# Constant products until the first operands, first two weight tiles by halves, x's last quarter behind tile 8's weights, its sum one tile later

## What is computed

```
mk, mv = rms_norm(mem, g) @ w_k, rms_norm(mem, g) @ w_v        # 256 memory tokens
x = x + token_mix(rms_norm(x))      # one input projection, convolution and gated linear attention, one output projection
x = x + cross_attn(rms_norm(x), mk, mv)
x = x + w_down @ relu(w_up @ rms_norm(x))**2
y = rms_norm(x)
```

## Time and profile before

| what | us |
|---|---|
| median of 3 runs | 1456.31 (1456.04 to 1456.56) |
| the profiled execution: its time, its span | 1456.2, 1454.5 |
| TensorE busy | 1437.2 (99%) |
| VectorE, ScalarE, GpSimd busy | 602.8, 458.0, 376.0 |

### The profile page before, as it was taken

The page is one execution under the profiler, slowest core; times in us unless marked ns, Lnnn a source line. Parts: engine busy times, 40 slices in busy tenths (PEclk is TensorE's granted clock), DMA queues, the critical chain, the costliest instruction groups (busy, mean ns, idle before and its releaser), DMA issues.

```text
span 1454.5 us, 22506 instructions
## 1 busy us (share of the span) xinstructions
PE 1437.2 (99%) x9501; PEld 1408.8 (97%) x9501; DVE 602.8 (41%) x688; ACT 458.0 (31%) x619; POOL 376.0 (26%) x296
## 2 busy tenths in 40 slices
PE   7999999999999999999999999999999999999998
PEld 7999999998999999889999999999999999999997
DVE  5669999987533555623322111221112211122124
ACT  7522253447522443312232200222002210023224
POOL 6642231125322211003222222222222222222220
PEclk9999999999999999999999999999999999999999
DMA  8511511002523411771111111111111111111113
GB/s 338 165 52 45 58 46 42 30 30 73 207 94 114 153 42 44 247 267 44 48 47 52 44 47 54 44 43 44 58 43 43 43 44 57 44 43 43 44 43 117
DMA packets 47357, 114.06 MB, mean 78 GB/s; under 512 B 7720, under 2 KB 23352, under 8 KB 45888
## 3 DMA queue, kind: packets, MB, share of 16 engines
q1 hardware_dynamic: 47296, 113.17, 24.3%
HBM read 100.85 MB, written 12.30 MB: 78 GB/s over the span
## 4 chain that ended last, share of the span: by engine, by line
PE 96%; DVE 3%; DMA 0%; ACT 0%; issue 0%; SPq 0%; DVEq 0%; ACTq 0%
PE ps L1214 59%; PE ps L1315 14%; PE ps L1609 5%; PE ps L1332 3%; PE m L1285 2%; PE ps L1643 2%; PE ps L1741 1%; PE ps L1562 1%; PE m L1522 1%; PE ps L1351 1%; DVE ps L1903 1%; PE ps L1622 1%; PE m L1437 1%; PE m L1586 1%; PE ps L1553 1%; PE m L1535 1%
## 5 line engine op out<-in xcount | busy, mean ns | idle before, releaser
L620 POOL TENSOR_TENSOR w_split<-w_raw,w_split 128x512 fp32r<-128x512 f32 x232 | 319.2, 1397 | 1041.6 <-ACT w_split L694 1041.5
L1214 PE MATMUL ps<-a_op,w_split 128*128 128x344 f32 x3168 | 499.4, 319 | 0.0
L1214 PEld LDWEIGHTS ps<-a_op,w_split 128*128 128x128 f32 x3168 | 497.8, 188 | 0.5 <-issue 0.5
L1214 PE MATMUL ps<-b_op,w_split 128*128 128x344 f32 x2304 | 362.6, 319 | 0.0
L1214 PEld LDWEIGHTS ps<-b_op,w_split 128*128 128x128 f32 x2304 | 361.7, 188 | 0.2
L1315 PE MATMUL ps<-a_op,w_split 128*128 128x344 f32 x1440 | 233.2, 321 | 0.0
L1315 PEld LDWEIGHTS ps<-a_op,w_split 128*128 128x128 f32 x1440 | 226.5, 188 | 1.7 <-issue 1.4
L694 ACT ACTIVATE w_split<-w_raw 128x1024 fp32r<-128x1024 f32 x117 | 122.7, 1051 | 255.2 <-PE ps L1214 246.0
L1903 DVE SCALAR_TENSOR_TENSOR ps<-conv_in,par,ps 128x1024 f32<-128x1024 f32 x116 | 149.7, 1291 | 3.6
L2289 DVE SCALAR_TENSOR_TENSOR tmp<-ps,rstd 128x1032 f32<-128x1032 f32 x32 | 39.5, 1233 | 215.1 <-PE ps L1214 203.2
L2299 DVE TENSOR_TENSOR x_res<-x_res,ps 128x1032 f32 x24 | 29.5, 1230 | 230.8 <-PE ps L1214 230.8
(11 more groups left out here) (255 smaller groups left out, 1100.7 us busy)
## 6 DMA issues: line engine op xcount, KB each, us to landing
w_raw<-in_wt SPq DMA_DIRECT2D x117, 512.0 KB, 3.5
cache_b<-in_cache_v SPq DMA_DIRECT2D x8, 1024.0 KB, 12.0
x_in<-in_x SPq DMA_DIRECT2D x4, 1032.0 KB, 9.2
x_spill<-x_res SPq DMA_DIRECT2D x8, 516.0 KB, 2.6
w_more<-in_wt SPq DMA_DIRECT2D x8, 512.0 KB, 7.1
cache_a<-in_cache_k SPq DMA_DIRECT2D x2, 2048.0 KB, 11.2
cache_b<-in_cache_k SPq DMA_DIRECT2D x2, 2048.0 KB, 11.9
x_res<-in_x SPq DMA_DIRECT2D x1, 3096.0 KB, 11.0
```

Of the source, the lines that this page charges most:

```text
L620: gp.tensor_tensor(split(t, slot)[:, 1, part, :], src, split(t, slot)[:, 0, part, :].bitcast(F32), ALU.subtract).then_inc(w_low_done, 1)
L1214: last = pe.matmul(ps[:, c0 // CB, 0:w], w_split[:, slot, wp, k, :], src[:, k, xp, c0:c0 + w], start=(k == 0 and j == 0), stop=(k == KT - ...
```

## The change

1. TensorE does eleven products of two constant tiles (ones and ident, 128x128, plain fp32) before the first real one. Their result is not read.
2. Tile 0's weights are loaded in two halves, with the parameters, and the memory's two halves between them; before, par, the whole of tile 0 and the memory's halves stood in this order. ScalarE copies tile 0's and tile 1's high parts in halves, with pieces of the memory's operand between them; a new semaphore, first_high, counts the first halves, and GpSimd starts tile 1's first half on it. VectorE makes tile 0's second half after four pieces of the memory's operand instead of three.
3. x's last quarter is issued after tile 8's weights instead of tile 7's, and ScalarE copies tile 8's high part before it squares x's pieces 6 and 7.
4. `x_sums` stands after tile 9 instead of tile 8, and ScalarE copies tile 12's high part before `norm_x` instead of after.

```
+            sp.dma_start(w_raw[:, 0, 0:KT // 2, :], WT[0][:, 0:KT // 2, :]).then_inc(first_half_loaded, 16)
             sp.dma_start(par[:, :], a["par"]).then_inc(params_loaded, 16)
...
-            load_w(0, 0, False)
-            for i in range(2):
-                sp.dma_start(m_raw[:, 4 * i:4 * i + 4, :], a["mem"][:, 4 * i:4 * i + 4, :]).then_inc(m_part[i], 16)
+            sp.dma_start(m_raw[:, 0:4, :], a["mem"][:, 0:4, :]).then_inc(m_part[0], 16)
+            sp.dma_start(w_raw[:, 0, KT // 2:KT, :], WT[0][:, KT // 2:KT, :]).then_inc(w_loaded[0], 16)
+            sp.dma_start(m_raw[:, 4:8, :], a["mem"][:, 4:8, :]).then_inc(m_part[1], 16)
...
-                if 5 <= t < 8:
-                    load_x(t - 4)
+                if t in (5, 6, 8):
+                    load_x((5, 6, 8).index(t) + 1)
...
-                gp.wait_ge(w_high_done, t + 1)
                 for k in (0, KT // 2):
+                    if isinstance(t, int) and t == 1 and k == 0:
+                        gp.wait_ge(first_high, 2)
+                    else:
+                        gp.wait_ge(w_high_done, t + 1)
...
-            w_high(0, 0)
+            def half_high(t, half):
+                part = slice(half * KT // 2, (half + 1) * KT // 2)
+                act.activation(w_split[:, t, 0, part, :], w_raw[:, t, part, :], ACT.Copy).then_inc((first_high, w_high_done)[half], 1)
...
+            act.wait_ge(first_half_loaded, 16)
+            half_high(0, 0)
             act.wait_ge(params_loaded, 16)
...
+            act.wait_ge(m_part[0], 16)
+            mem_high(0, 1, 2, 3)
+            act.wait_ge(w_loaded[0], 16)
+            half_high(0, 1)
+            act.wait_ge(m_part[1], 16)
+            mem_high(4, 5)
+            act.wait_ge(w_loaded[1], 16)
+            half_high(1, 0)
+            mem_high(6, 7)
+            half_high(1, 1)
             w_high(2, 0)
...
             square_x(5)
             w_high(7, 1)
+            w_high(8, 0)
             square_x(6)
-            w_high(8, 0)
             square_x(7)
-            for t in range(9, 12):
+            for t in range(9, 13):
                 w_high(t, t % 2)
             norm_x()
-            w_high(12, 0)
...
             pe.wait_ge(consts_ready, 1)
+            for _ in range(11):
+                pe.matmul(M[1][:, 0:P], ones[:, :], ident[:, :], start=True, stop=True)
             for n_kv in range(T_IN):
                 kv_product(n_kv)
                 if n_kv == 2:
                     sums(1, 0, MEM)
-                if n_kv == 8:
+                if n_kv == 9:
                     x_sums()
...
-            dve.wait_ge(w_high_done, 1)
+            dve.wait_ge(first_high, 1)
             first_low(0)
             for k in range(KT):
-                if k == 3:
+                if k == 4:
+                    dve.wait_ge(w_high_done, 1)
                     first_low(KT // 2)
```

More of the change, by code:

```diff
@@ L244, in build @@
         w_high_done = sem("w_high_done")
+        first_high = sem("first_high")
+        first_half_loaded = sem("first_half_loaded")
         w_low_done = sem("w_low_done")
@@ L709, in _, with mem_high @@
             act.activation(small[:, 129:130], small[:, 128:129], ACT.Sqrt)
-            w_high(0, 0)
-            act.wait_ge(params_loaded, 16)
[L712 to L717, removed]
+            def half_high(t, half):
+                part = slice(half * KT // 2, (half + 1) * KT // 2)
+                act.activation(w_split[:, t, 0, part, :], w_raw[:, t, part, :], ACT.Copy).then_inc((first_high, w_high_done)[half], 1)
+            def mem_high(*ks):
+                for k in ks:
+                    act.activation(m_op[:, k, 0, :], m_raw[:, k, :], ACT.Copy,
+                                   scale=par[:, G_MEM + k:G_MEM + k + 1]).then_inc(operand_high, 1)
+            act.wait_ge(first_half_loaded, 16)
+            half_high(0, 0)
+            act.wait_ge(params_loaded, 16)
+            act.wait_ge(m_part[0], 16)
[8 more added lines that the diff above has]
+            half_high(1, 1)
             w_high(2, 0)
```

## The result

The changed kernel takes 1462.75 us (median of 6 runs, 1461.72 to 1463.08) against 1456.43 for the kernel before on the same chip (6 runs, 1456.04 to 1457.17): a ratio of 1.0041, interval 1.0032 to 1.0051, 6.3 us slower. The prediction was 1457.5, at most 1458.8. The profiled execution took 1462.9.

What follows compares the result with a forecast made beforehand. TensorE bounds the kernel, busy 1437.2 of 1454.5 us. Terms: 0 (constants) - 0.74 (clock, first operand) + 2.8 (x_sums behind tile 9) - 0.84 (VectorE's slack) = +1.3 with rounding, so 1457.5 us, range 1455.3 to 1458.8.

Steps and rivals of the forecast that it cites:

- GpSimd begins tile 1's low part at about 10.0 instead of 11.05 (first_high): Before the memory's sum: GpSimd starts tile 1 earlier, its second half done at 12.7, so tile 1 ends at 14.5.
- It lands at about 5.92: Start: the memory's first half, with 256 KB less queued before it, lands 0.64 us earlier, at 5.92 instead of 6.56.
- The eleven constant products. ... I cost them at nothing: Start: the products take 2.5 to 4.9 us, hidden in TensorE's wait for its first operands; cost 0.
- Between 60 us and the end I find no other change: After tile 16 begins: nothing more gained or lost, so the shift at tile 16 counts for the whole kernel.
- The memory's sum as the gate at 18.1: After tile 2: VectorE's reduction of the memory's squares ends at 18.1, so TensorE waits 0.8 us there.
- g: How much earlier than before TensorE gets past the memory's sum; above 2.0 us needed for a faster kernel.
- the weights rival: New wait for weights at tile 7 or 9, or x's last quarter: 0.3 to 1.5 us above forecast; chance 0.12.
- the same time: At the memory's sum: with the clock not raised, TensorE would arrive at 18.2, against a sum ready at 18.1.
- The late sum: x_sums after tile 9 begins at 38.4 instead of 36.29, delaying VectorE's row and kv_evac(7) by 2.1 us.
- VectorE's slack: Before kv_evac(7), ahead of tile 16: VectorE is idle 0.84 us, from 58.12 to 58.96, which absorbs that much delay.
- Tile 8's weights: x's last quarter behind them makes them ready 1.1 us earlier, no wait; otherwise 0.2 us would be lost at tile 8.
- the one of 0.74: Term for clock and earlier first operand: TensorE leaves the memory's sum 0.74 us earlier, 18.1 instead of 18.84.

Runs made afterwards that it cites:

- Experiment 5: The changed kernel with GpSimd's first half of tile 1 waiting for all of the memory's low pieces: 1460.02 us, ratio to before 1.0028.
- experiment 9: The kernel before with tile 0 loaded by two half-size transfers, one after the other: 1457.93 us, ratio 1.0009.
- experiment 6: The kernel before with tile 0's load in halves, parameters and memory's first half between; ScalarE copies tile 0 whole: 1458.30 us, ratio 1.0014.
- experiment 1: The kernel before with the eleven constant products alone: 1457.19 us, ratio 1.0005.
- experiment 11: The kernel before with 88 already-met TensorE waits ahead of the first product: 1457.27 us, ratio 1.0005.
- experiment 2: The kernel before with only x's last quarter behind tile 8's weights and x_sums after tile 9: 1458.07 us, ratio 1.0012.
- experiment 12: The changed kernel with its loads as in the kernel before, tile 0 whole: 1461.62 us, ratio to before 1.0039.
- experiment 3: The changed kernel without the constant products and the edits on x's last quarter and x_sums: 1459.16 us, ratio to before 1.0015.
- experiment 4: The changed kernel with x_sums back after tile 8 and tile 12's copy back behind norm_x: 1461.25 us, ratio to before 1.0028.
- experiment 7: The kernel before with eleven constant products and x's last quarter and its squares behind tile 8's weights: 1457.21 us, ratio 1.0006.
- experiment 10: The kernel before with three 512-column constant products and x's last quarter behind tile 8's weights: 1455.72 us, ratio 0.9995.

## Why the prediction was wrong, by its own steps

- **"GpSimd begins tile 1's low part at about 10.0 instead of 11.05 (first_high)", costed as a gain, is the step that failed most.** It let GpSimd subtract while VectorE still had pieces 6 and 7 to do: 1.28 and 1.50 us instead of 0.48 each. GpSimd in fact began at 11.34, but VectorE's last two pieces, at 11.61, were later still; by the prediction's own times (ScalarE's pieces 6 and 7 from 9.8 to 10.6) they would have met too. TensorE starved for it and its clock fell. Experiment 5 takes the overlap away and is 2.7 us faster, of which about 2.0 are the edit's: 0.7 of idle time between pieces and 1.3 of clock (27 matmuls in 4.6 us instead of 3.3). The prediction gave the rule for it (the Trainium skill, SBUF — State Buffer, "Who interferes with whom": two SBUF inputs on VectorE against a GpSimd instruction that reads SBUF) and applied it to x_low at 52 us, where it changed little, and not to the pieces at 11 us, which have two SBUF inputs too. By that rule, the trace agrees: both pieces end 0.3 us after the GpSimd instruction beside them, at 12.9 and 14.3. In the kernel before GpSimd began at 11.05 and VectorE's last piece ended at 11.05: there was no slack to move it by.
- **"It lands at about 5.92"**: 7.32. Twelve of its sixteen shares landed by 5.7, as worked out from the rate, the last four from 7.2. The rate of whole transfers (408 GB/s) does not hold for halves: experiments 9 and 6 lose 1.4 to 1.5 us on the memory's second half with the transfers alone. The reason is open.
- **"The eleven constant products. ... I cost them at nothing"**: right for the array, wrong for the program. They lengthen TensorE's program by 44 instructions; a 16 KB load of it moves into the keys' transfer 480 us later and costs 1.6 us there in the changed kernel (1.0 and 1.1 in the traces of experiments 1 and 11, whose medians are 0.8 and 0.75 slower). "Between 60 us and the end I find no other change" is the sentence that failed.
- **The memory's sum as the gate at 18.1**: never reached. The sum of squares was ready at 19.2, TensorE came at 21.76. g, which the forecast had at +0.74 and the weights rival at less, was -2.9. The prediction held that without a raised clock TensorE would come to the sum at "the same time", so that the clock was worth almost nothing; it rose, fell, and mattered.
- **The late sum**: right, and its size too. It costs 2.0 - g at VectorE's slack, less the 0.3 us by which the three x_low were shorter. By the formula, 59.71 + 2.0 - g, tile 16 is due at 64.6 in the changed kernel (64.33), 61.0 in experiment 2 (60.65), 62.3 in 5 (62.04), 62.9 in 12 (62.61); with the sum in its old place, by 59.71 - g, at 62.7 in experiment 3 (62.66) and 63.7 in 4 (63.73).
- **Tile 8's weights**: right, and worth more than the 0.2 us it had for them. From the memory's sum to x's sum it is 17.45 us before and 17.46 in experiment 7, but 18.00 in experiment 1: 0.55 lost.

The sum as it was: 2.9 (late data, starved pieces, fallen clock, less what the constants saved) + 1.7 (the late sum) + 1.6 (the keys) + 0.5 (the last products at the low clock) = 6.7 of span. Of the forecast's terms the one of 0.74 went to -2.9, which is 3.7 of the 5.4 us between 1.3 and 6.7; the keys are 1.6 and the end 0.5, and the late sum was 0.3 cheaper. No single experiment adds all of these up, and the runs of kernels with a fallen clock spread by 1.4 us (the changed kernel) to 6.2 (experiment 12), so the first term is that of the profiled execution.

## What to carry to other kernels

When an edit lets one engine start earlier, look up what the engine beside it does in just that stretch: work of GpSimd and VectorE that each hid behind a wait can block each other once both are on time, and a TensorE that starves for its operands can lose its high clock again just when the real work begins, with constants ahead of it or without (the changed kernel, experiment 3). A constant filler is work for the array but also length of program: make it of few wide instructions (experiment 10), and look in the trace at where the program's own loads fall. What follows a moved step on a second engine (here a whole row of VectorE's) is charged in full once its slack, 0.84 us here, is used up.

## What the runs showed of the hardware that was not expected

- 88 waits that are already met, ahead of the first product, made the kernel 0.75 us slower; its trace has 1.1 us of loss at 489 us, where a 16 KB load of TensorE's program has moved from 489.7 to 486.4.
- Two transfers of 256 KB in a row land what follows them 1.4 us later than one of 512 KB.
- With the same instructions ahead of it, the clock came up at different times in different executions: the first products of the kernel before went at 0.213 us until 13.4, those of experiment 2 until 11.7. The 0.76 us between their memory's sums (18.84 and 18.08) is this, with data and edits the same up to there.
